# Sums of squares of the first block's norms: adding tiles on GpSimd ahead of TensorE

## The reference

```python
def rms_norm(x, g):
    y = xf * lax.rsqrt(jnp.mean(xf * xf, axis=-1, keepdims=True) + RMS_EPS)
    return (y * g)

def first_block(x, ...):
    for l in range(DEPTH):                     # DEPTH = 2
        h = modulate(rms_norm(x, norm_ffn1[l]), sh1, sc1)
        x = x + 0.5 * g1 * swiglu(h, ffn1_w_in[l], ffn1_w_out[l])
        h = modulate(rms_norm(x, norm_mix[l]), sh2, sc2)
        x = x + g2 * token_mix(h, ...)
        h = modulate(rms_norm(x, norm_ffn2[l]), sh3, sc3)
        x = x + 0.5 * g3 * swiglu(h, ffn2_w_in[l], ffn2_w_out[l])
    return rms_norm(x, final_norm)

# second_block, first lines of layer 0
h_x = modulate_2(rms_norm_2(x, g[0]), ...)
h_c = modulate_2(rms_norm_2(ctx, g[0]), ...)   # ctx: 256 tokens of context
```

## Time and profile before

| what | value |
|---|---|
| time, median of 3 runs | 2228.17 us |
| lowest and highest run | 2224.69, 2229.52 us |
| span of the profiled execution (first to last instruction) | 2222.6 us |
| PE busy | 2155.5 us, 97% |
| DVE busy | 1674.6 us, 75% |
| ACT busy | 990.5 us, 45% |
| POOL busy | 31.1 us, 1% |
| mean granted PE clock, share of full speed | 0.987 |

### The profile page before, as it was taken

How to read it: one execution, slowest core, us unless ns; L and a number is a source line. 1 busy time by engine, 2 the same in 40 slices (tenths; PEclk the granted TensorE clock), 3 DMA queues, 4 the chain that set the end, 5 groups by cost and what they waited for, 6 DMA issues and landing times.

```text
span 2222.6 us, 36384 instructions
## 1 busy us (share of the span) xinstructions
PE 2155.5 (97%) x15539; PEld 1993.2 (90%) x15539; DVE 1674.6 (75%) x2327; ACT 990.5 (45%) x1331; POOL 31.1 (1%) x33
## 2 busy tenths in 40 slices
PE   7999999999999999999999899999999999999998
PEld 7999987999999998799998678888888887889998
DVE  6999877788798877778776774777776568987563
ACT  4534434534443443443344664422222348764442
POOL 0000000000000000000000000000000001110000
PEclk9999999999999999999999999999999999999999
DMA  9999744798789864467774102254465232133662
GB/s 322 317 330 309 248 133 150 242 316 298 264 284 305 302 202 153 142 196 248 236 228 142 36 4 74 80 186 155 156 221 189 76 114 69 48 122 127 223 191 76
DMA packets 338631, 417.47 MB, mean 188 GB/s; under 512 B 9274, under 2 KB 263208, under 8 KB 338472
## 3 DMA queue, kind: packets, MB, share of 16 engines
q1 hardware_dynamic: 335360, 411.84, 56.2%
q10 hardware_dynamic: 3112, 3.33, 0.5%
HBM read 414.09 MB, written 1.05 MB: 187 GB/s over the span
## 4 chain that ended last, share of the span: by engine, by line
PE 46%; DVE 7%; ACT 3%; issue 2%; POOL 0%; DVEq 0%; ACTq 0%
PE pb L623 45%; ACT wh L1461 1%; DVE wl L2100 1%; DVE T L2108 1%; PE pb L1289 1%; DVE ACC L2108 1%; DVE SM L2694 1%; DVE RS L2192 0%; DVE Hl L2108 0%; DVE L_y L2108 0%; ACT A_P L1935 0%; DVE L_y L2100 0%; ACT L_y L1462 0%; DVE L_y L2815 0%; DVE L_u L2108 0%
## 5 line engine op out<-in xcount | busy, mean ns | idle before, releaser
L623 PE MATMUL pb<-Hh,wh 128*128 128x256 f32 (+1 forms) x2624 | 795.5, 304 | 13.8 <-DVE wl L2100 5.4
L623 PE MATMUL pb<-Hl,wh 128*128 128x256 f32 (+1 forms) x2624 | 779.3, 297 | 0.0
L623 PE MATMUL pb<-Hh,wl 128*128 128x256 f32 (+1 forms) x2624 | 774.7, 297 | 0.0
L2100 DVE TENSOR_TENSOR wl<-raw,wh 128x2048 fp32r<-128x2048 f32 (+3 forms) x271 | 600.9, 2222 | 179.9 <-ACT wh L1461 179.1
L1461 ACT ACTIVATE wh<-raw 128x2048 fp32r<-128x2048 f32 (+3 forms) x271 | 502.2, 1855 | 357.6 <-PE pb L623 259.0
L623 PEld LDWEIGHTS pb<-Hh,wh 128*128 128x128 f32 x2624 | 504.6, 192 | 33.5 <-issue 9.6
L623 PEld LDWEIGHTS pb<-Hl,wh 128*128 128x128 f32 x2624 | 504.9, 192 | 15.3 <-issue 2.2
L623 PEld LDWEIGHTS pb<-Hh,wl 128*128 128x128 f32 x2624 | 501.9, 192 | 12.8
L623 PE MATMUL pb<-Bh,wh 128*128 128x256 f32 (+1 forms) x1376 | 420.1, 305 | 7.1 <-DVE Y L2100 2.5
L623 PE MATMUL pb<-Bl,wh 128*128 128x256 f32 (+1 forms) x1376 | 413.5, 300 | 0.0
L623 PE MATMUL pb<-Bh,wl 128*128 128x256 f32 (+1 forms) x1376 | 413.4, 300 | 0.0
(11 more groups left out here) (256 smaller groups left out, 2113.9 us busy)
## 6 DMA issues: line engine op xcount, KB each, us to landing
raw<-in_ada_w_dram SPq DMA_DIRECT2D x126, 1024.0 KB, 5.5
raw<-in_ffn_w_in_dram SPq DMA_DIRECT2D x88, 1024.0 KB, 6.7
raw<-in_mlp_w_dram SPq DMA_DIRECT2D x64, 1024.0 KB, 5.3
raw<-in_ffn_w_out_dram SPq DMA_DIRECT2D x32, 1024.0 KB, 6.5
raw<-in_mix_w_in_dram SPq DMA_DIRECT2D x22, 1024.0 KB, 5.7
raw<-in_ffn_w_out_dram SPq DMA_DIRECT2D x16, 768.0 KB, 4.6
raw<-in_attn_w_qkv_dram SPq DMA_DIRECT2D x12, 1024.0 KB, 6.2
raw<-in_lru_w_in_dram SPq DMA_DIRECT2D x10, 1024.0 KB, 5.1
```

Source lines behind the costliest of these rows:

```text
L623: return e.matmul(o, l, r, start=st, stop=sp, skip_group_check=True)
L2100: return e.tensor_tensor(o, a, b, f)
```

## The change

Class `Folded` takes the place of `Sums` at the six norms inside and at the end of the first block. POOL adds the squares of tiles 1 to 5 to that of tile 0 (tiles 1 to 3 for the pair), one tensor_tensor add each, in place in slot 4. PE sums the folded tile and the ones that are left (6 and 7; 4 to 7 for the pair) in one go, at the place where the next phase's `sums.add()` stood; nothing is summed between the units any more. The slots are handed out anew (`FOLD_SLOT`): ACT waits for POOL's adds before it writes a slot again, and for the last tile of the pair for PE's read of tile 4. For the context POOL adds all eight tiles into one, and PE sums that one, at step (1, 0) in place of (0, 3). ACT's root follows at (1, 1) in place of (1, 0), DVE's reciprocal at (1, 2) in place of (1, 1). The very first norm of the kernel keeps `Sums`. Three semaphores are merged into one (`made`). The core of the diff:

```diff
+FOLD_SLOT = (4, 5, 6, 7, 5, 6, 7, 5)
+FOLDED = {256: 6, 512: 4}
...
+            class Folded:
+                def __init__(self, n):
+                    self.n, self.p = n, bank(SUMS_BANK, "rs.sqrt", n // 256)
+
+                def add(self):
+                    q0, f0 = E.n["sq"], E.n["fold"]
+                    E.up("sq", 8)
+                    E.up("fold", FOLDED[self.n] - 1)
+                    for i, kt in enumerate((0, *range(FOLDED[self.n], 8))):
+                        if i:
+                            E.wait_ge("sq", q0 + kt + 1)
+                        else:
+                            E.wait_ge("fold", f0 + FOLDED[self.n] - 1)
+                        E.mark(mm(self.p[:, 0:self.n], ONES, T[:, FOLD_SLOT[kt], 0:self.n], i == 0, kt == 7), "fold.read")
...
             def ffn(l, seg, sums, first=None):
...
-                        if first and (c, j) == (0, 3):
+                        if first and (c, j) == (1, 0):
                             csum = Sums(256)
-                            for kt in range(8):
-                                E.wait_ge("sq", E.up("sq"))
-                                mm(csum.p[:, 0:256], ONES, c_slot(kt), kt == 0, kt == 7).then_inc(sems["sq.read"], 1)
+                            E.up("sq", 8)
+                            E.wait_ge("fold", E.up("fold", 7))
+                            E.mark(mm(csum.p[:, 0:256], ONES, c_slot(0), True, True), "fold.read")
...
                     if c == last:
-                        sums = Sums(512 if l and seg else 256)
+                        sums = Folded(512 if l and seg else 256)
...
                         fm("fo", "fo", hid_at(b), 256, hid_need, said="x", by=2)
-                        if c == last and m:
-                            sums.add(2 * m)
...
                     fm("mo", "mo", hid_at(0), 256, mo_need, fresh=m == 0, said="x", by=2)
                     if m == 0:
-                        sums = Sums(256)
-                    else:
-                        sums.add(2 * m)
+                        sums = Folded(256)
...
+            def folded_square(kt, src, n, gained=False):
+                folded = FOLDED[512 if gained else 256]
+                if kt == 0:
+                    E.up("fold", folded - 1)
+                    E.up("fold.read", 9 - folded)
+                if kt == 6:
+                    act(SM[:, 25:26], KM[:, K_ONE:K_ONE + 1], ACT.Sqrt)
+                if kt > 3 and kt - 3 < folded:
+                    E.wait_ge("fold", E.n["fold"] - (folded - 1) + kt - 3)
+                elif kt > 3:
+                    E.wait_ge("fold.read", E.n["fold.read"] - (9 - folded) + kt - 3 - folded + 2)
...
                 for kind, c, j in mlp_steps(FFN_PAIRS):
...
-                        if first and (c, j) == (1, 0):
-                            E.wait_ge("sq.read", nsq[0])
+                        if first and (c, j) == (1, 1):
+                            E.wait_ge("fold.read", E.up("fold.read"))
                             act(RS[:, 256:512], PB[SUMS_BANK][:, 0:256], ACT.Sqrt, bias=EPSC, scale=1.0 / D).then_inc(sems["rs.sqrt"], 1)
...
-                        if first and (c, j) == (1, 1):
+                        if first and (c, j) == (1, 2):
                             E.wait_ge("rs.sqrt", E.up("rs.sqrt"))
                             E.step(e.reciprocal(RS[:, 256:512], RS[:, 256:512]))
...
+            def add_squares(dst, src, k):
+                E.wait_ge("sq", k)
+                E.wait_ge("fold", E.n["fold"])
+                E.mark(e.tensor_tensor(dst, dst, src, ALU.add), "fold")
+
+            def folded(n):
+                q0 = E.n["sq"]
+                E.up("sq", 8)
+                for kt in range(1, FOLDED[n]):
+                    add_squares(T[:, 4, 0:n], T[:, FOLD_SLOT[kt], 0:n], q0 + kt + 1)
+
+            E.up("sq", 8)
+            q0 = E.up("sq", 8) - 8
+            for kt in range(1, 8):
+                add_squares(c_slot(0), c_slot(kt), q0 + kt + 1)
...
             for l in range(2):
+                folded(256)
                 for b in range(2):
                     chosen(l, b)
                     barred(l, b)
+                folded(256)
+                folded(512 if l else 256)
```

More of the change, by code:

```diff
@@ L325, in build @@
         names += ["c.t", "c.hi", "c.h", "rs.w", "xn", "cx.read", "qc.hi", "qc.lo"]
-        names += ["taken", "w.hi", "cols", "mod", "sq", "sq.read", "rs.sqrt", "h.t", "h.hi", "h", "x",
-                  "g.read", "u.read", "hid.hi", "hid", "su.read", "ct.read", "l_d0", "l_d1", "cols0", "sgu.w", "rope", "rope.arg", "decay", "decay.exp", "idb",
+        names += ["taken", "w.hi", "cols", "mod", "sq", "sq.read", "fold", "fold.read", "rs.sqrt", "h.t", "h.hi", "h", "x",
+                  "g.read", "u.read", "hid.hi", "hid", "su.read", "ct.read", "l_d0", "l_d1", "cols0", "sgu.w", "rope", "made", "decay", "decay.exp",
                   "rp.read", "rot.read", "rope.q", "wi.read", "lq.read", "sel.in", "sel", "bias.in", "bias", "vv.read", "mu.read", "mv.read",
@@ L876, in ffn @@
                 mods((0, 0, l, seg), (0, 0, l, seg + 1))
-                sums.add()
+                if seg or l:
+                    sums.add()
                 if between:
@@ L1218, in _ @@
             sums.add()
-            SQUARES["first"] = E.n["sq"]
+            SQUARES["first"] = E.n["fold.read"]
             cx_rest(between)
@@ L1275, in score2 @@
                 if c == 0:
-                    E.wait_ge("band", 1)
+                    E.wait_ge("made", 4)
                     far = slice(128 - 128 * b, 256 - 128 * b)
@@ L1509, in root_mean @@
                     E.wait_ge("sq.read", nsq[0])
+                    E.wait_ge("fold.read", E.n["fold.read"])
                     E.wait_ge("dve.step", 1)
@@ L1542, in squares @@
                     E.wait_ge("x", E.up("x"))
-                    square(kt, XC[:, kt, 0:256], 256, gained)
+                    folded_square(kt, XC[:, kt, 0:256], 256, gained)
             cxs = [0]
@@ L1744, in turns @@
             def turns():
-                E.wait_ge("rope.arg", 1)
+                E.wait_ge("made", 2)
                 act(SIN[:, :], M_an[:, :], ACT.Sin).then_inc(sems["rope"], 1)
-                E.wait_ge("rope.arg", 2)
+                E.wait_ge("made", 3)
                 act(COS[:, :], M_kk[:, :], ACT.Sin).then_inc(sems["rope"], 1)
@@ L2481, in start_rest @@
                 own()
-                E.mark(ts(M_an[:, :], M_an[:, :], 3.1415925, -3.1415925, ALU.min, ALU.max), "rope.arg")
-                E.wait_ge("rope.arg", 1)
+                E.mark(ts(M_an[:, :], M_an[:, :], 3.1415925, -3.1415925, ALU.min, ALU.max), "made")
+                E.wait_ge("made", 2)
                 E.step(ts(M_kk[:, :], M_an[:, :], -1.0, None, ALU.mult, None))
@@ L2487, in start_rest @@
                 own()
-                E.mark(ts(M_kk[:, :], M_kk[:, :], -1.0, float(np.float32(np.pi / 2)), ALU.mult, ALU.add), "rope.arg")
+                E.mark(ts(M_kk[:, :], M_kk[:, :], -1.0, float(np.float32(np.pi / 2)), ALU.mult, ALU.add), "made")
             for l in range(2):
@@ L2625, in _ @@
             E.step(tt(S_GX, S_GX, vt("n_fin"), ALU.mult))
-            E.wait_ge("sq.read", SQUARES["first"])
+            E.wait_ge("fold.read", SQUARES["first"])
             E.step(ts(RS[:, 0:256], PB[SUMS_BANK][:, 0:256], EPS / D, EPS * EPS, ALU.mult, ALU.add))
```

14 lines of the change are left out of this document (9 added, 5 removed).

## The result

The changed kernel takes 2214.77 us, the median of 7 runs (2206.94 to 2219.01); the kernel before took 2224.69 us beside it (7 runs, 2220.85 to 2229.52). The ratio is 0.9954 with a 95% interval of 0.9937 to 0.997, so 10.2 us faster, with 6.7 to 14.0 for the interval. Against the 2228.17 us that the forecast started from it is 13.4 us, and the forecast was 2217.6. The profiled span is 2211.4 us at a mean granted clock of 0.989, against 2222.6 at 0.987.

The account below looks back on a forecast made before the run. PE was taken to bound the norms and DVE the stretch from the context's sum to 195 us. Terms -1.7 - 8.6 - 2.6 + 2.3 = -10.6 us, from 2228.2 to 2217.6 us; 8-in-10 range 2211.5 to 2223.5.

Parts of the forecast that it names:

- The bound by place: Whole kernel: PE's work counts in full at the norms; from the context's sum to 195 us DVE sets the end.
- Four norms at 2.15 each, 8.6: Four later 256-column norms: five tiles of 0.43 us leave PE at each, 8.6 us faster in all.
- just in time, taken as 0: Late norms: the fold is ready as PE asks for it, 0 to 0.4 us late at worst, counted as 0.
- the rival by which the gain is taken back: Whole kernel: the weight stream is the true limit, PE only reaches its next wait sooner; 2228 less at most 2; chance 0.06.
- The first norm, -1.7: Layer 0, ffn1 to mix: folded tile fits PE's wait for square 6, only four tiles count, 1.7 us faster.
- The late fold: Rival at five norms: DVE's split delays the last adds and PE waits 1 us at each; 2222.6 us; chance 0.10.
- the forecast's own sign that the timing of the adds is wrong: At the norms: a PE wait ended by POOL before the folded tile would show the adds' timing wrong; none was expected.
- The pair, -2.6: 512-column norm ending the first block: eight tiles become five at 0.86 us each, 2.6 us faster.
- The reckoning that square 7 is hidden: At the pair: square 7 waits for PE's read of tile 4 but is hidden, with 0.9 us to spare.
- The context's sum, +2.3: Near 79 us: seven adds hold DVE 0.4 us each, less 0.5 us slack, so 2.3 us later at 195 us.
- against the rival: At the context's sum: PE, not DVE, sets the pace, so its 3.0 us are gained too; 2212.3 us; chance 0.10.
- Clock: Rival: longer PE waits at 195 us and the first norm bring one to three more clock drops; 2219.3 to 2222.7; chance 0.10.

Follow-up runs that it names:

- fold last: The changed kernel's norms with the context's sum of the kernel before, folded tile summed last instead of first: 2207.41 us, ratio 0.992; again 2209.91 us, ratio 0.9935.
- the two experiments on order and count: Norms' part without the context's: folded tile summed last (ratio 0.992, again 0.9935); five tiles folded instead of six, three for the pair (2211.87 us, ratio 0.9937).
- the norms alone: The changed kernel's six folded norms with the context's sum as in the kernel before: 2212.43 us, ratio 0.9944; again 2210.38 us, ratio 0.9937.
- the context alone: The kernel before with only the context's part (seven POOL adds, one tile on PE, root one pair later): 2226.96 us, ratio 1.0005.

## Why the prediction came out right, and where its steps did not

*The bound by place* was right. PE's work was worth its length at the norms and nothing at the context's sum.

*Four norms at 2.15 each, 8.6.* Second -2.25 and fifth -2.14 (read between traces of equal half clock: 140.61 with fold last and 137.01 in the changed kernel's repeat, against 142.86 and 139.15), third -1.77, fourth -1.78: 7.9. The step that was mis-sized is "just in time, taken as 0", with 0 to 0.4 us given as possible. The add was sized at 0.5 to 0.6 us from half of a 512-column one and the hand-over at 0.33; they are 0.74 and 0.14, so the pitch of 0.8 to 0.9 was nearly right. The add that meets the split ends 0.6 us behind it where 0.5 was taken. Small errors on a margin of zero: the lateness cost 0.37 us at two norms, as the two experiments on order and count show. That these two keep 1.77 us of their 2.15 in every trace with this fold also answers the rival by which the gain is taken back.

*The first norm, -1.7.* Measured -0.9 against the first trace of before and -1.5 against its repeat. Instead of fitting into the wait for square 6, the fold ended that wait, 1.31 us long: the last four adds began 0.22 us into a full split (249.91 to 252.19 us), and the first two of them took 3.93 us. With the fold last PE waited there as long for square 6, so the room that the forecast saw was not there either way. The late fold was among the rivals, at 1 us for each of five norms; it came at four, with 0.2 to 0.8 us at the first and 0.4, 0.4 and 0.8 at the third, the fourth and the pair. It was also the forecast's own sign that the timing of the adds is wrong, a wait ended by POOL ahead of the folded tile, and it stands at the first norm and at the pair.

*The pair, -2.6.* Measured -1.20. The size of a tile, 0.86 us, was right. The lateness of the fold takes 0.84 of it back, as fold last gives back. The rest is a wait for a residual update on DVE, at 1148.99 us, which the kernel before does not have; it is 0.34 us of idle time, and the matmul starts 0.50 later than its step would have it. It stands at 1147.74 with fold last too. The reckoning that square 7 is hidden holds here.

*The context's sum, +2.3.* Measured at the restart +3.2 and +4.0 in two traces, +3.9 alone, two of the three beyond the +3.4 given as the worst. The mechanism is right, the size was low: 0.46 for each add in place of 0.4, since every operation of DVE beside the adds is held, those with a single SBUF input too (0.29 to 0.72 us), for which the forecast had no row. The slack of 0.5 us that I took off was not wholly used up either: DVE still waits 0.3 us for ACT's halves between 82 and 196 us, and 1.4 in the repeat, whose restart is the later one. PE was not the bound there, against the rival.

The Trainium skill (SBUF — State Buffer, "SBUF: two separate sides") names as users of the shared pair also VectorE operations in a two-port mode, which this single-input case may be; no run here separates the modes. That a lock lasts "for the whole instruction" is not what the rows show: 0.43 us of operation and 0.74 of add would make a period of 1.17, and it is 0.88.

*The sum.* -0.9 -7.9 -1.2 +3.2 = -6.8 us where -10.6 was forecast, for the parts that the change is made of. The first trace is 11.2 us shorter: 4.4 of that are clock and start (start -1.3, second norm's stretch -0.5, fifth's -1.9, behind the pair -0.7), which the repeats show to come and go. The timed interval, 6.7 to 14.0 us, holds the forecast well inside and -6.8 at its very edge.

Is the rest of the timed 10.2 us luck of the clock? The granted clock of each execution is on record, and it does not look so: its mean is 0.9884 over eight executions of the changed kernel and 0.9888 over 65 of the kernel before. A fit to 150 executions of all kernels, with one price for the time that the clock took (0.72 us for each us), puts the changed kernel 10.6 us under before (9.3 to 11.9), the norms alone 12.1, the fold last 14.2, and the context alone 0.7 us above it, each good to some 1.3 us. It takes the chips of the different runs as equal. So the total of -10.6 came out, but its terms were 3.8 us too good, and some 4 us of gain stand in no part that I read. The restart and the first norm are the likeliest place, as they scatter by 1.5 us and there are only two traces of the kernel before; that is not shown. That the two amounts match is luck.

*Clock.* The longer wait at 197 us did not cost more: the clock is 0.83 over 10 us there as before. A new drop stands behind the wait at 81 us, for 3.4 us, and since DVE sets that stretch it is not seen in the restart. The drops near 350, 905 and 1230 us vary more from run to run than between the kernels.

*Open.* Where those 4 us lie. And whether the changed kernel is slower than its norms alone: the traces say 2 to 3.4 us at the restart, the timed intervals overlap, and the fit above leaves 1.4 us, with 1.5 either way.

## What to carry to other kernels

Before work goes to an idle engine, ask at each place which engine's work ends last: taking 3 us from an engine that is 100% busy bought nothing where its neighbour set the pace, and the adds that replaced it cost 3. Size a moved chain by its pitch (length and hand-over) beside the longest operation that can hold it up, and put what comes last at the end of the consumer's order: a fold whose lateness cost 0.4 us cost nothing once it was summed last, except where the square summed in its place came just as late. Where runs scatter by 4 us, compare intervals between fixed events in stretches at full clock; they repeat to 0.03 us. Then add the parts up against the timed whole: a total that fits does not show that its terms do.

## What the runs showed of the hardware

- A GpSimd add of 128x256 f32 takes 0.74 us in a row of seven (the first 0.90), one each 0.88 us beside DVE work; 2.54 us and a little more when it starts within a 2.28 us split on DVE.
- One such add holds a DVE operation of 256 columns up by 0.43 to 0.55 us; one with a single SBUF input is held as well (0.29 to 0.72). An add of a constant tile to itself (0.61 to 0.68 us) holds one of 256 columns up by 0.30 to 0.47, and such adds hold a two-input one of 512 columns up by 0.23 and a split of 2048 columns by 0.41.
- Seven adds beside DVE moved each of DVE's first nine splits behind them by 3.0 to 3.2 us. A PE lighter by 3 us moved the first three by nothing.
- These kernels have two starts, some 6 us apart: in 3 of 13 profiled executions the later one, with 17.1 us at half clock. Two of the kernels showed both.
